# Norm sums gathered on VectorE, layers written out without loops, and two weight units loaded ahead of each layer

## The reference, cut to what matters

```python
h = rmsnorm(x, norm_mix_pre)
proj = h @ w_in
...
mixed = jax.nn.sigmoid(gate_a) * y_att + jax.nn.sigmoid(gate_b) * y_rw
x = x + rmsnorm(mixed @ w_out, norm_mix_post)
h = rmsnorm(x, norm_ffn_pre)
u = causal_dwconv(h @ w_up, conv_w, conv_b)
x = x + rmsnorm((jax.nn.gelu(ua) * ub) @ w_down, norm_ffn_post)
e = p_i @ w_ple
x = x + rmsnorm(jax.nn.sigmoid(x @ w_ple_gate) * e, norm_ple)
```

## Time and profile before

| What | Value |
|---|---|
| median of 3 runs | 4268.4 us (4267.18 to 4272.71) |
| the profiled execution: its own time, its span | 4264.91 us, 4263.1 us |
| mean granted TensorE clock | 0.967 of full |
| PE busy, PEld busy | 3971.9 us (93%), 3239.1 us (76%) |
| DVE, ACT, POOL busy | 2122.7, 1676.3, 1685.7 us |
| first product matmul of the four layers | at 33.73, 1431.44, 2825.71, 3547.31 us |
| instruction DMA (queues q8 and q14) | 3.92 and 0.81 MB for 70941 instructions |

### The profile page before, as it was taken

One profiled execution on the slowest core, in us unless ns is written; L12 is line 12 of the kernel. 1 busy time (PEld: TensorE's weight loads), 2 busy tenths in 40 slices (PEclk: granted clock), 3 DMA queues, 4 the chain that ended last, 5 costly groups with the idle time before them and its releaser, 6 DMA issues. The chain is left out here.

```text
span 4263.1 us, 70941 instructions
## 1 busy us (share of the span) xinstructions
PE 3971.9 (93%) x29464; PEld 3239.1 (76%) x29464; DVE 2122.7 (50%) x2976; ACT 1676.3 (39%) x2803; POOL 1685.7 (40%) x904
## 2 busy tenths in 40 slices
PE   7999988989999799998898999989999998999998
PEld 5787867867887677786687788767878876777887
DVE  6677674149863577776513986335231112523112
ACT  4444434344334445443433433435232223523222
POOL 3434312424445344341242444524434443443443
PEclk9999999989999899999998999989999998999999
DMA  3111113324532211111232454211222222122222
GB/s 124 42 42 46 51 60 107 104 72 175 191 130 85 87 37 46 51 51 60 97 104 70 169 192 139 92 63 46 98 80 95 98 84 82 49 94 80 98 99 79
DMA packets 109634, 380.59 MB, mean 89 GB/s; under 512 B 13168, under 2 KB 13552, under 8 KB 108656
## 3 DMA queue, kind: packets, MB, share of 16 engines
q1 hardware_dynamic: 99072, 357.89, 24.6%
q10 hardware_dynamic: 10224, 17.97, 1.1%
HBM read 360.04 MB, written 15.78 MB: 88 GB/s over the span
## 5 line engine op out<-in xcount | busy, mean ns | idle before, releaser
L247 POOL TENSOR_TENSOR Wlo<-raw,Whi 128x1024 fp32r<-128x1024 f32 x554 | 1374.2, 2485 | 2154.4 <-ACT Whi L235 2154.2
L192 PE MATMUL ps<-hh,Whi 128*128 128x512 f32 x2864 | 1161.2, 405 | 89.1 <-POOL Wlo L247 26.1
L192 PE MATMUL ps<-hl,Whi 128*128 128x512 f32 x2864 | 1127.3, 394 | 0.0
L192 PE MATMUL ps<-hh,Wlo 128*128 128x512 f32 x2864 | 1125.9, 393 | 0.0
L235 ACT ACTIVATE Whi<-raw 128x1024 fp32r<-128x1024 f32 x554 | 583.1, 1054 | 769.4 <-PE ps L192 635.7
L192 PEld LDWEIGHTS ps<-hh,Whi 128*128 128x128 f32 x2864 | 545.0, 190 | 225.8 <-issue 52.5
L192 PEld LDWEIGHTS ps<-hl,Whi 128*128 128x128 f32 x2864 | 545.8, 191 | 115.8 <-issue 8.6
L192 PEld LDWEIGHTS ps<-hh,Wlo 128*128 128x128 f32 x2864 | 544.4, 190 | 117.2
L192 PE MATMUL ps<-gh,Whi 128*128 128x512 f32 x864 | 341.0, 395 | 7.6 <-issue 5.7
L192 PE MATMUL ps<-gh,Wlo 128*128 128x512 f32 x864 | 337.9, 391 | 0.0
L192 PE MATMUL ps<-gl,Whi 128*128 128x512 f32 x864 | 337.4, 391 | 0.0
(11 more groups left out here) (358 smaller groups left out, 5977.6 us busy)
## 6 DMA issues: line engine op xcount, KB each, us to landing
raw<-in_stream SPq DMA_DIRECT2D x554, 512.0 KB, 3.3
ada<-in_ada SPq DMA_DIRECT2D x96, 512.0 KB, 4.1
park_x<-xT SPq DMA_DIRECT2D x2, 2048.0 KB, 10.6
park_yh<-yh ACTq DMA_DIRECT2D x16, 256.0 KB, 2.0
park_yl<-yl ACTq DMA_DIRECT2D x16, 256.0 KB, 2.3
xT<-park_x SPq DMA_DIRECT2D x2, 2048.0 KB, 7.7
yrh<-park_yh ACTq DMA_DIRECT2D x16, 256.0 KB, 7.7
yrl<-park_yl ACTq DMA_DIRECT2D x16, 256.0 KB, 7.8
```

The source lines that it names most:

```text
L192: last = pe.matmul(ps, left[a](k), right[c](k), start=start and k == 0 and i == 0, stop=stop and k == n - 1 and i == 2)
L247: pool.tensor_tensor(b["Wlo"][:, u % SLOTS], b["raw"][:, u % RAW], b["Whi"][:, u % SLOTS].bitcast(F32), SUB) \
```

## The change

Three things are changed together.

1. **Norm sums.** In the five norms that come out of a product (`n2`, `n4`, `n5` of the first stack, `n2`, `nx` of the second), ACT writes the square of tile 0 to a new buffer `sacc`, DVE adds the squares of tiles 1 to 5 to it, and PE sums over partitions only three things, all after the last product: `sacc`, and the squares of tiles 6 and 7. In `n4` and second stack `nx` ACT squares one tile behind the product, not two, and DVE's add for a tile stands behind its work on the product two tiles later.
2. **Loops.** The layers are written out (`for layer in range(LAYERS)` in place of `nc.Fori`). The parameters of all layers are loaded in the prologue; the modulation stays in SBUF (`mods`), with no `park_mods`.
3. **Lead units.** Units 0 and 1 of a layer are loaded, and their `Whi` and `Wlo` made, at the end of the layer ahead (the first layer's in the prologue, behind its root). Slots rotate on over the boundary.

In `mods_pe` a one-column matmul with 128 weight columns becomes two with 64 each.

```diff
+def summed_square_act(act, s, b, name, i, src):
+    if i >= 3:
+        act.wait_ge(s[name + "_ac"], i - 2)
+    act.activation(b["sq"][:, i % 2] if i else b["sacc"][:], src, ACT.Square).then_inc(s[name + "_sq"], 1)
+
+def square_sum_dve(dve, s, b, name, i):
+    if 1 <= i <= KD - 3:
+        dve.wait_ge(s[name + "_sq"], i + 1)
+        if i >= 2:
+            dve.wait_ge(s[name + "_ac"], i - 1)
+        dve.tensor_tensor(b["sacc"][:], b["sacc"][:], b["sq"][:, i % 2], ADD).then_inc(s[name + "_ac"], 1)
+
+def summed_squares_pe(pe, s, b, name):
+    pe.wait_ge(s[name + "_ac"], KD - 3)
+    column_sums(pe, b, b["sacc"], True, False)
+    for i in (KD - 2, KD - 1):
+        pe.wait_ge(s[name + "_sq"], i + 1)
+        last = column_sums(pe, b, b["sq"][:, i % 2], False, i == KD - 1)
     last.then_inc(s[name + "_ss"], 1)
...
@@ Ring.take
-        pe.wait_ge(self.s["w_lo"], self.u)
+        if self.u > LEAD:
+            pe.wait_ge(self.s["w_lo"], self.u - LEAD)
...
@@ HighParts
-        self.s, self.b, self.freed, self.u = s, b, freed, 0
+        self.s, self.b, self.freed, self.u = s, b, freed, LEAD
-        while self.u < min(n, len(self.freed)):
+        while self.u < min(n, len(self.freed) + self.b["leads"]):
...
@@ mods_pe
-        pe.matmul(b["ps"][:, b["norm_bank"], 4 * g + j:4 * g + j + 1], b["macc"][:, g % 2, j * P:j * P + P], b["c"]("ones")[:, 0:1],
-                  start=True, stop=True).then_inc(s["m_p"], 1)
+        for u in range(2):
+            last = pe.matmul(b["ps"][half(u), b["norm_bank"], 4 * g + j:4 * g + j + 1],
+                             b["macc"][:, g % 2, j * P + 64 * u:j * P + 64 * u + 64], b["c"]("ones")[:, 0:1], start=True, stop=True)
+        last.then_inc(s["m_p"], 1)
...
@@ project_pe (n2 of both stacks, n5)
-        if after:
-            after(m)
+    summed_squares_pe(pe, s, b, name)
...
@@ ffn_pe (n4)
-            if key[2] == OPEN:
+            if key[2] == KD - 1:
                 pe.wait_ge(s["mods_v"], 1)
-                norm_sum_pe(pe, s, b, "n4", 0, KD)
-            sums_behind(pe, s, b, "n4", key[2], 2)
+                summed_squares_pe(pe, s, b, "n4")
...
@@ ffn_dve (n4) and, alike, second_dve (nx)
             down_dve(dve, s, b, key[1], key[2])
+            if key[1] == PARTS1 - 1:
+                square_sum_dve(dve, s, b, "n4", key[2] - 2)
...
@@ first_block
-        with nc.Fori(0, LAYERS) as layer:
+        for layer in range(LAYERS):
+            enter_layer(b, layer, stream[layer], stream[layer + 1] if layer + 1 < LAYERS else stream_after[0])
...
-                    sp.dma_start(b["par"][:], params[bass.ds(layer, 1)].rearrange("l p n -> (l p) n")).then_inc(s["par_in"], 16)
-                    stream_loads(sp, s, b, stream, layer, 0, 2)
                     sp.dma_start(b["park_x"], b["xT"][:]).then_inc(s["x_out"], 16)
-                    stream_loads(sp, s, b, stream, layer, 2, AT_ATT + 8)
+                    stream_loads(sp, s, b, LEAD, AT_ATT + 8)
...
+                    stream_loads(sp, s, b, AT_E + 2, UNITS1 + b["leads"])
...
@@ first_block, DVE
                     mixed_low_dve(dve, s, b)
+                    for i in range(1, KD - 2):
+                        square_sum_dve(dve, s, b, "n2", i)
                     norm_dve(dve, s, "n2", b)
...
@@ prologue, SP
+                for u in range(LEAD):
+                    sp.dma_start(b["raw"][:, u], units[u]).then_inc(s["w_in"], 16)
+                for layer in range(LAYERS):
+                    sp.dma_start(b["par"][:, layer], params[layer]).then_inc(s["par_in"], 16)
+                    sp.dma_start(b["par2"][:, layer], params2[layer]).then_inc(s["par_in"], 16)
...
@@ prologue, ACT and POOL
                 norm_root_act(act, s, b, "nx", KD, D)
+                act.wait_ge(s["w_in"], 16 * LEAD)
+                for u in range(LEAD):
+                    act.activation(b["Whi"][:, u], b["raw"][:, u], ACT.Copy).then_inc(s["w_hi"], 1)
+
+            @block.gpsimd
+            def _(pool):
+                for u in range(LEAD):
+                    pool.wait_ge(s["w_hi"], u + 1)
+                    pool.tensor_tensor(b["Wlo"][:, u], b["raw"][:, u], b["Whi"][:, u].bitcast(F32), SUB).then_inc(s["w_lo"], 1)
```

More of the change, by code:

```diff
@@ L144, in norm_act, with column_sums @@
     norm_root_act(act, s, b, name, n, dim)
+def summed_square_act(act, s, b, name, i, src):
[8 more added lines that the diff above has]
+        dve.tensor_tensor(b["sacc"][:], b["sacc"][:], b["sq"][:, i % 2], ADD).then_inc(s[name + "_ac"], 1)
+def column_sums(pe, b, src, first, end):
+    for c in range(BLK):
+        for u in range(2):
+            last = pe.matmul(b["ps"][half(u), b["norm_bank"], c:c + 1], src[:, c * P + 64 * u:c * P + 64 * u + 64],
+                             b["c"]("ones")[:, 0:1], start=first and c == 0, stop=end, skip_group_check=True)
+    return last
 def norm_sum_pe(pe, s, b, name, i, n):
     pe.wait_ge(s[name + "_sq"], i + 1)
[L150 to L153, removed]
+    column_sums(pe, b, b["sq"][:, i % 2], i == 0, i == n - 1).then_inc(s[name + "_ss"], 1)
+def summed_squares_pe(pe, s, b, name):
[4 more added lines that the diff above has]
+        last = column_sums(pe, b, b["sq"][:, i % 2], False, i == KD - 1)
     last.then_inc(s[name + "_ss"], 1)
@@ L243, in low_parts, with stream_loads @@
 def low_parts(pool, s, b, first, end):
-    for u in range(first, end):
[L246 to L256, removed]
+    for u in range(max(first, LEAD), end):
+        pool.wait_ge(s["w_hi"], u - LEAD + 1)
+        slot = weight_slot(b, u)
+        pool.tensor_tensor(b["Wlo"][:, slot], b["raw"][:, raw_slot(b, u)], b["Whi"][:, slot].bitcast(F32), SUB) \
+            .then_inc(s["w_lo"], 1)
+def stream_loads(sp, s, b, first, end, beside=None):
+    for u in range(first, end):
+        if u >= RAW + LEAD:
+            sp.wait_ge(s["w_lo"], u - RAW - LEAD + 1)
+        units, total = b["units"], b["units"].shape[0]
+        sp.dma_start(b["raw"][:, raw_slot(b, u)], units[u] if u < total else b["next_units"][u - total]) \
             .then_inc(s[f"w_in{u % RAW}"], 16)
@@ L1675, in split_pair, with project_pe @@
                 last.then_inc(done, 1)
[L1678 to L1685, removed]
+def project_pe(pe, s, b, ring, done, copied, ready, name):
     for m in range(KD):
@@ L1925, with enter_layer, leave_layer, first_block @@
 UNITS1 = AT_PG + KD
-def first_block(nc, b, stream, params, ple, ada, positions):
+def enter_layer(b, layer, units, next_units):
+    b["layer"], b["units"], b["next_units"] = layer, units, next_units
+    b["leads"] = LEAD if next_units is not None else 0
+def leave_layer(b):
+    total = b["units"].shape[0]
+    b["slot0"], b["raw0"] = (b["slot0"] + total) % SLOTS, (b["raw0"] + total) % RAW
+def first_block(nc, b, stream, stream_after, ple, ada, positions):
     names = ["tb2" + x for x in TABLE_SEMS] + ["tab_out", "n1_sp"] + \
-        [f"ada_in{i}" for i in range(ADA)] + ["md_v", "m_p", "mods_v", "mods_out"] + [f"w_in{i}" for i in range(RAW)] + ["w_hi", "w_lo", "par_in", "ple_in", "zeroed", "x_out", "x_back"] + \
+        [f"ada_in{i}" for i in range(ADA)] + ["md_v", "m_p", "mods_v"] + [f"w_in{i}" for i in range(RAW)] + ["w_hi", "w_lo", "ple_in", "zeroed", "x_out", "x_back"] + \
         norms("n2", "n3", "n4", "n5", "nx") + [n + x for n in ("h1", "h2") for x in SPLIT_SEMS] + \
@@ L1939, in sb @@
             b[name] = into.enter_context(nc.sbuf_tensor(name, [P, *shape], dt))
-        sb(ctx, "par", NPAR1)
         sb(ctx, "hh", KD, TOK, dt=F32R)
         sb(ctx, "hl", KD, TOK, dt=F32R)
[L1944 to L1947, removed]
+        b["p"] = lambda name, i: b["par"][:, b["layer"], PAR1[name] + i:PAR1[name] + i + 1]
         with ExitStack() as c:
@@ L1951, in first_block @@
         with ExitStack() as c:
[L1952 removed]
+            for name, *shape in (("t1", 2, TOK), ("t2", 2, TOK), ("sq", 2, TOK), ("sacc", TOK)):
                 sb(c, name, *shape)
@@ L2659, in second_block @@
         assert len(freed) == UNITS2
-        with nc.Fori(0, LAYERS) as layer:
+        for layer in range(LAYERS):
+            enter_layer(b, layer, stream[layer], stream[layer + 1] if layer + 1 < LAYERS else None)
             with nc.Block() as block:
```

136 lines of the change are left out of this document (72 added, 64 removed).

## The result

The changed kernel takes 4224.3 us (median of 4 runs, 4221.7 to 4226.9), the kernel before 4270.6 us (4 runs, 4267.2 to 4273.0). The ratio is 0.9899, 95% interval 0.9887 to 0.9912: 43 us faster (38 to 48), where 75 were forecast, and outside the range of 4176 to 4216. The two medians lie 46 us apart; gains over the kernel before, and their intervals, are taken from the ratios.

The account below looks back on a forecast made before the run. The prediction took PE, busy 93% of the span, as the bound. Its terms, 49 + 2.5 + 30.5 - 1 - 5.0 - 0.6 = 75.4 us gained, gave 4189.5 to 4193; it forecast 4191, range 4176 to 4216 us.

Parts of the forecast that it names:

- Norm sums in the streams: Sums leaving PE's product streams in five norms: 0.77 us each plus first waits, 49 us gained (bounds 38 to 50).
- sweeps of 5.44 us per unit: Sign that the sums had left the product sweeps: 5.44 us per unit instead of 6.23.
- the low clock: First 3 to 5 us of each layer's products run at 1.2 GHz: expected unchanged, + 0 (bounds - 5 and + 5).
- Norm sums with their tails: Sums leaving the streams gain 49.4 us; longer norm ends after the last product cost 5.0 us.
- Adds on DVE: 50 adds of squares, about 0.75 us each, 37 us of DVE, fit its idle time in the sweeps: cost nothing.
- Loops: At the starts of layers two and four the branch back falls away: 3.6 us each.
- Early units: Layer starts: units 0 and 1 loaded and split beforehand, worth 23.3 us of the starts' 30.5 without the loops' 7.2.
- The starts: First products of the four layers come earlier by 1.9, 11.8, 6.3 and 10.5 us: 30.5 us gained.
- Modulation sums: Sixteen 64-column instructions replace eight of 128 columns in each of 24 sums: 2.5 us gained (0 to 7).
- Unit 2 behind `park_x`: After layer starts, the later-issued unit 2 might stall PE: 1 us lost in all (bounds none, or 3 at two layers).
- The streams have another bound: Rival: in the sweeps ACT, POOL or loads hold PE, half of 49 us is lost, 4216 us; chance 0.10.
- Straight code: Rival: written-out layers make instructions arrive late, 3.6 us a stall, 4335 us with 40 stalls; chance 0.03.

Follow-up runs that it names:

- e1_after_aligned: Changed kernel plus 288 unused bytes a partition ahead of `hh_2`, putting the second stack's moving tiles at the weights' place modulo 512: 4183.7 us, ratio 0.9801.
- e2_before_shifted: Kernel before plus 224 unused bytes a partition ahead of `hh_2`, giving the second stack the changed kernel's distance between weights and moving tiles: 4302.0 us, ratio 1.0078.
- e5_before_unrolled: Kernel before with only the two loops over the layers written out: 4262.2 us, ratio 0.9986.
- e8_aligned_tails: Changed kernel with second-stack buffers aligned by unused bytes, and adds and a sum of `n4` and `nx` moved ahead of the last down product: 4186.9 us, ratio 0.9811.

## Why the prediction was wrong

**The step that failed** is one that the prediction never wrote down as a step. Under "Norm sums in the streams" it priced a sum against "two distances of 0.227", and among its signs it named "sweeps of 5.44 us per unit". It took the distance between two product matmuls for a property of the chip that no part of this change touches. It depends on where the operands lie, and the change moves `Whi` and `Wlo`; the sum has no term for that, so it stood at nothing. In the second stack some 4,700 matmuls (3 x 1053 of `hh` and `hl`, 3 x 512 of `gh` and `gl`) came to a distance of 224 bytes modulo 256 from their weights: 4,700 x 6.7 ns = 31 us. e1_after_aligned takes it back (41 us between its median and the changed kernel's, 42 by the two ratios), and e2_before_shifted makes it alone (33 by the ratio).

About 7 of the 38.2 us by which the second stack of e1_after_aligned is shorter in the profiled executions (4224.4 - 2776.06 against 4182.5 - 2772.37) are not in these 31. They lie where products are more than 0.26 us apart, mostly at the low clock (about 0.44 us from start to start): I count 75 such distances there, 108 in the changed kernel, 106 in the kernel before. Without the two in each that are over 1 us, they exceed 0.227 us by 13.6, 20.7 and 17.7 us in sum, and 20.7 - 13.6 = 7.1 is what was missing. So e1_after_aligned owes some of its 85 us to the clock and not to the place of its buffers. Why these counts differ, no run here settles.

**The rest held**, most of it closely:
- *Norm sums with their tails*: 49.4 less 5.0 forecast, 48 (41 to 54) measured alone. The tails: `n4` was 0.7 to 0.9 us longer, as sized (0.7); `nx` at the end of layer four 0.5 in the changed kernel and 0.9 in e1_after_aligned (1.5 was taken); `n2` and `n5` nothing (0.1 was taken). Each sum in a sweep gives 0.79.
- *Adds on DVE*, costed at nothing: 50 adds in 42.9 us, 859 ns each. 42 of them take 0.68 to 0.69 us, eight meet a `Wlo` and take 1.2 to 2.6; no product waits for one in a sweep.
- *Loops*: 7.2 forecast, 6 (2 to 10) measured, with 4.5 and 3.6 us in the two timelines.
- *Early units*: 23.3 forecast; 28 against units behind `park_x`, about 22 against the old order.
- *The starts*: 1.8 us in layer one, then (from reciprocal to first product, as forecast) 12.2, 6.6 and 10.4 us in the changed kernel, where 1.9, 11.8, 6.3 and 10.5 were forecast.
- *Modulation sums*: 2.5 forecast. The time that the 24 put between the products around them fell from 38.7 to 37.8 us, to 36.2 in e1_after_aligned. One that waits for nothing gives 0.15 us, as forecast; one that waits for DVE takes 2.2 us as before. What the halves gave, the wait took where there is one: counted at the weight load, 24.4 us in 14 waits where there had been 18.6 in 13.
- *Unit 2 behind `park_x`*: no stall appeared; `park_x` lands in 7.2 us.

With the distance taken out, the forecast of 75 us stands against 85 (79 to 90) in e1_after_aligned. The parts come to 48 + 6 + 22 = 76, and modulation sums to 1 to 2.5. Low-clock distances of the second stack gave some 4 us more (17.7 less 13.6), while the forecast had put the low clock at + 0, with bounds of - 5 and + 5; the last few us no run assigns. The forecast's own sum has a slip: its 5.0 for the tails already holds the 0.6 of `n2` and `n5` (0.6 + 3.0 + 1.4), and the sum takes 0.6 off again, so its terms come to 76.0.

**The rivals.** "The streams have another bound" gave 4216, near the 4224 measured, and for a wrong reason: PE waits for no weights in the sweeps, and DVE idles 4.25 us a product. Straight code brings no new stalls: the "issue" waits before a product's weight load are 87.5 us after 91.5, and e5_before_unrolled, where only the loops are written out, is 6 us faster.

**What the trace of before could have told.** Its second stack already had both speeds side by side, same engine, same line, same shape:

```profile
L192 PE MATMUL ps<-gl,Whi 128*128 128x512 f32 x488 | 189.9, 389 | 0.0
...
L192 PE MATMUL ps<-aol,Whi 128*128 128x512 f32 x64 | 25.3, 396 | 0.0
```

`aol` stood at 480 modulo 512 and its weights at 32. Two durations for one shape are a question, and the diff moved just what answers it.

## What to carry to other kernels

When one instruction shape has two durations in a trace, find out why before using either as a constant: here it was the place of the operands, and moving an allocation changed 4,700 matmuls on which the diff has no line. For streams of 128 x 128 float32r weights against 512 columns, put moving tiles and weights at the same place modulo 256 bytes; an unused buffer does it. And when a part is measured alone on the old kernel and gives as much as the whole change, look for a loss that the rest brings.

## What the runs showed of the hardware that was not expected

- The distance between float32r matmuls of 128 x 128 by 512 columns depends on the start of the moving tile against the weights modulo 256 bytes: 0.2267 us at 0, 0.2290 at 64, 0.2323 to 0.2342 at the other multiples of 32 that were tried, with nothing else running. 4 bytes cost more (0.2366) than 32 (0.2334), and with 256 columns there was no loss (0.1199 at 0, 0.1187 at 128).
- The way back of a loop on all engines cost 4.5 and 3.6 us at its two places (the starts of layers two and four in e5_before_unrolled).
- A VectorE add of two SBUF tiles that begins while POOL makes a `Wlo` ends 0.54 us behind it (2.47 and 1.72 us in place of 0.68 in e8_aligned_tails), so its time depends on where in the `Wlo` it begins.
